# Moving the exponentials and the shares of a tile's expert choice to later rows of the plan

## What is computed

```python
q = (ht @ peer_wq).reshape(T, PEER_HEADS, PEER_DK)            # T = 512, 8 heads
s1, s2 = q[..., :half] . peer_k1, q[..., half:] . peer_k2     # 128 scores each
v1, i1 = lax.top_k(s1, 16);  v2, i2 = lax.top_k(s2, 16)
cand = (v1[..., :, None] + v2[..., None, :]).reshape(T, 8, 256)
sc, pos = lax.top_k(cand, 16)
experts = (e1 * 128 + e2)                                     # e1, e2 from i1, i2 by pos
gates = jax.nn.softmax(sc, axis=-1)
a = jax.nn.gelu(einsum("ckd,cd->ck", peer_u[experts], h)) * gates
out = einsum("ck,ckd->cd", a, peer_v[experts])
```

## Time and profile before

| | us |
|---|---|
| runs before: median of 3 (lowest, highest) | 2980.7 (2978.4, 2987.61) |
| the profiled execution, its own time | 2978.2 |
| its span, first to last instruction | 2976.5 |
| TensorE busy in the span | 2824.8 (95%) |
| VectorE busy | 2235.7 (75%) |
| ScalarE busy | 1481.7 (50%) |
| GpSimd busy | 582.0 (20%) |

### The profile page before, as it was taken

One profiled execution on the slowest core, in us unless ns is written; L12 is line 12 of the kernel. 1 busy time (PEld: TensorE's weight loads), 2 busy tenths in 40 slices (PEclk: granted clock), 3 DMA queues, 4 the chain that ended last, 5 costly groups with the idle time before them and its releaser, 6 DMA issues.

```text
span 2976.5 us, 37320 instructions
## 1 busy us (share of the span) xinstructions
PE 2824.8 (95%) x13639; PEld 2359.7 (79%) x13639; DVE 2235.7 (75%) x3019; ACT 1481.7 (50%) x1990; POOL 582.0 (20%) x460
## 2 busy tenths in 40 slices
PE   5989987999999989999999999899999999999998
PEld 3666756888888857776777789899999998888887
DVE  6465546888888863696964599999777658888886
ACT  3433235888888843544552333555665633333332
POOL 0200111111111100000000000233333324444442
PEclk7999998999999999999999999999999999999999
DMA  7544635999999833232334324688998999999995
GB/s 305 171 160 146 212 137 205 368 372 367 363 360 352 324 140 128 86 114 89 117 106 149 114 86 142 236 293 308 322 319 310 326 337 358 368 364 357 362 371 174
DMA packets 201771, 737.90 MB, mean 248 GB/s; under 512 B 24432, under 2 KB 77808, under 8 KB 145008
## 3 DMA queue, kind: packets, MB, share of 16 engines
q1 hardware_dynamic: 124656, 497.12, 46.3%
q0 software_dynamic: 55056, 170.87, 16.7%
q10 hardware_dynamic: 21872, 67.48, 5.9%
HBM read 666.61 MB, written 93.91 MB: 256 GB/s over the span
## 4 chain that ended last, share of the span: by engine, by line
PE 64%; DVE 13%; issue 4%; ACT 2%; DMA 1%; ACTq 0%; DVEq 0%; SPq 0%; POOLq 0%
PE PS L544 55%; DVE wlo L1891 3%; PE PS L1145 2%; PE PS L1011 1%; PE PS L1023 1%; DVE hf L2700 1%; ACT whi L1221 1%; PE PS L850 1%; DVE oh L2674 1%; DVE hf L2688 1%; ACT HH L1861 1%; DVE cand L2640 1%; DVE cand L2642 1%; PE PS L1002 1%; DVE sS L2727 0%
## 5 line engine op out<-in xcount | busy, mean ns | idle before, releaser
L1891 DVE TENSOR_TENSOR wlo<-raw,whi 128x2048 fp32r<-128x2048 f32 x392 | 894.2, 2289 | 311.9 <-ACT whi L1221 270.9
L1221 ACT ACTIVATE whi<-raw 128x2048 fp32r<-128x2048 f32 x392 | 750.7, 1916 | 371.5 <-PE PS L544 317.3
L544 PE MATMUL PS<-HH,whi 128*128 128x512 f32 (+1 forms) x2056 | 787.8, 383 | 20.1 <-ACT HH L1257 10.1
L544 PE MATMUL PS<-HH,wlo 128*128 128x512 f32 (+1 forms) x2056 | 750.6, 365 | 0.0
L544 PE MATMUL PS<-HL,whi 128*128 128x512 f32 (+1 forms) x2056 | 750.3, 365 | 0.0
L544 PEld LDWEIGHTS PS<-HH,whi 128*128 128x128 f32 x2056 | 390.5, 190 | 78.1 <-issue 20.4
L544 PEld LDWEIGHTS PS<-HL,whi 128*128 128x128 f32 x2056 | 390.6, 190 | 46.6 <-issue 7.7
L544 PEld LDWEIGHTS PS<-HH,wlo 128*128 128x128 f32 x2056 | 389.3, 189 | 43.3
L544 PE MATMUL PS<-whi,HH 128*128 128x512 f32 (+1 forms) x896 | 350.6, 391 | 11.1 <-DVE HL L2730 5.8
L544 PE MATMUL PS<-whi,HL 128*128 128x512 f32 (+1 forms) x896 | 346.8, 387 | 0.0
L544 PE MATMUL PS<-wlo,HH 128*128 128x512 f32 (+1 forms) x896 | 346.8, 387 | 0.0
(11 more groups left out here) (434 smaller groups left out, 3891.9 us busy)
## 6 DMA issues: line engine op xcount, KB each, us to landing
raw<-in_moe_dram SPq DMA_DIRECT2D x192, 1024.0 KB, 7.2
raw<-in_u_units_dram SPq DMA_DIRECT2D x64, 1024.0 KB
raw<-in_v_units_dram SPq DMA_DIRECT2D x64, 1024.0 KB
raw<-in_w_in_dram SPq DMA_DIRECT2D x44, 1024.0 KB
raw<-in_w_ada_dram SPq DMA_DIRECT2D x24, 1024.0 KB, 20.1
acts_dram<-sS ACTq DMA_DIRECT2D x64, 384.0 KB
gates_dram<-XT ACTq DMA_DIRECT2D x24, 1024.0 KB
sS<-acts_dram SPq DMA_DIRECT2D x42, 384.0 KB
```

Of the source, the lines that this page charges most:

```text
L544: ins = t.matmul(dst, a, b, start=(first and n == 0), stop=(last and n == 2))
L1221: a.inc(a.e.activation(m.whi[p % HRING][:, :, :], m.raw[RAW_SLOT[load_of(p)]][:, :, :], ACT.Copy), "hi", p)
L1891: v.inc(v.e.tensor_tensor(m.wlo[h][:, :, :], m.raw[RAW_SLOT[load_of(p)]][:, :, :], m.whi[h][:, :, :].bitcast(F32), ALU.subtract), "lo_v", p)
```

## The change

The share (r = 9) leaves the list of choice steps, which has nine steps for a tile instead of ten. The planner puts the exponential of a tile three rows after its subtraction (`EXP_AFTER`) and its share four rows after it (`SHARE_AFTER`), as entries 3 and 4 of a row. ScalarE does the exponential after the row's gate steps instead of before them; VectorE does the share after the row's gate steps and before its choice steps. The gate steps hang on the row of the share instead of that of the last choice step. The rule that a tile's first step may not stand in the row in which the tile before it was finished is gone.

```diff
--- before.py
+++ after.py
@@ -157,7 +157,8 @@
 
 
 CHOICE_ORDER = (1, 0, 2, 3)
-CHOICE_NS = (1500, 4600, 4600, 2000, 3400, 3400, 3400, 3400, 800, 700)
+CHOICE_NS = (1500, 4600, 4600, 2000, 3400, 3400, 3400, 3400, 800)
+EXP_AFTER, SHARE_AFTER, SHARE_NS = 3, 4, 700
 N_PAIR = 4 * 16 + 12 * 4
 CHOICE_STEPS = len(CHOICE_NS)
 N_GATE = 32 * (NT - TD // 128)
@@ -172,15 +173,16 @@
 
 
 def peer_schedule():
-    up, chosen, a, b, c = [], {}, 0, 0, 0
+    up, chosen, shared, a, b, c = [], {}, {}, 0, 0, 0
     tensor, vector = 0, FOUND_NS
     for n in range(128):
-        row = ([], [], [])
+        row = ([], [], [], [i for i in chosen if n == chosen[i] + EXP_AFTER], [i for i in shared if n == shared[i]])
         tensor += 4200
         vector = max(vector, tensor - 4200) + 1150
-        first = chosen.get(TD // 128, n)
+        vector += SHARE_NS * len(row[4])
+        first = shared.get(TD // 128, n)
         while (b * (LAST_GATE - first) < GATE_STEPS * (n - first) and b < GATE_STEPS and len(row[1]) < 2
-               and (b >= N_GATE or n > chosen.get(TD // 128 + b // 32, n))):
+               and (b >= N_GATE or n > shared.get(TD // 128 + b // 32, n))):
             row[1].append(b)
             b += 1
             tensor += 1100
@@ -192,13 +194,11 @@
             c += 1
         while a < CHOICE_STEPS * NT and vector < tensor + 2000:
             i, r = choice_of(a)
-            if r == 0 and a and n == chosen[choice_of(a - 1)[0]]:
-                break
             row[0].append(a)
             vector += CHOICE_NS[r]
             a += 1
             if r == CHOICE_STEPS - 1:
-                chosen[i] = n
+                chosen[i], shared[i] = n, n + SHARE_AFTER
         up.append(row)
     assert a == CHOICE_STEPS * NT and b == GATE_STEPS
     down = [list(range(c + (256 - c) * min(n, 124) // 124, c + (256 - c) * min(n + 1, 124) // 124))
@@ -1778,12 +1778,10 @@
     a.mark("scored")
 
 
-def act_choice_step(a, m, step):
-    i, r = choice_of(step)
-    if r == 8:
-        a.wait_ge("gsub", i)
-        dst = m.act0[:, :] if i * 128 < TD else m.gt[:, i, :, :].rearrange("p h k -> p (h k)")
-        a.inc(a.e.activation(dst, dst, ACT.Exp), "gexp5", i)
+def act_choice_exp(a, m, i):
+    a.wait_ge("gsub", i)
+    dst = m.act0[:, :] if i * 128 < TD else m.gt[:, i, :, :].rearrange("p h k -> p (h k)")
+    a.inc(a.e.activation(dst, dst, ACT.Exp), "gexp5", i)
 
 
 def act_gate_step(a, m, step):
@@ -1844,10 +1842,10 @@
         u, ci = divmod(n, 2)
         if ci == 0:
             act_high(a, m, FIRST["u_units"] + u + HRING - 1)
-        for step in PEER[n][0]:
-            act_choice_step(a, m, step)
         for step in PEER[n][1]:
             act_gate_step(a, m, step)
+        for i in PEER[n][3]:
+            act_choice_exp(a, m, i)
         for step in PEER[n][2]:
             act_gather_step(a, m, step)
         activation(n)
@@ -2652,13 +2650,18 @@
             v.inc(e.tensor_copy(m.IDX[:, :].rearrange("p (h k) -> p h k", h=8), m.e12[:, :, :]), "index")
         v.inc(e.tensor_tensor(G3, m.sc16[:, :, :], bass.AP(m.sc16, 0, [[128, 128], [16, 8], [0, 16]]),
                               ALU.subtract), "gsub", i)
-    elif r == 9:
-        v.wait_ge("gexp5", i)
-        v.inc(e.tensor_reduce(m.gs[:, :], G3, AX.X, ALU.add), "pick")
-        v.own()
-        v.inc(e.reciprocal(m.gs[:, :], m.gs[:, :]), "pick")
-        v.own()
-        v.inc(e.tensor_tensor(G3, G3, bass.AP(m.some, 16, [[32, 128], [1, 8], [0, 16]]), ALU.mult), "gt", i)
+
+
+def dve_choice_share(v, m, i):
+    e = v.e
+    dst = m.act0[:, :] if i * 128 < TD else m.gt[:, i, :, :].rearrange("p h k -> p (h k)")
+    G3 = dst.rearrange("p (h k) -> p h k", h=8)
+    v.wait_ge("gexp5", i)
+    v.inc(e.tensor_reduce(m.gs[:, :], G3, AX.X, ALU.add), "pick")
+    v.own()
+    v.inc(e.reciprocal(m.gs[:, :], m.gs[:, :]), "pick")
+    v.own()
+    v.inc(e.tensor_tensor(G3, G3, bass.AP(m.some, 16, [[32, 128], [1, 8], [0, 16]]), ALU.mult), "gt", i)
 
 
 def dve_gate_step(v, m, step):
@@ -2709,6 +2712,8 @@
             dve_low(v, m, FIRST["u_units"] + n // 2 + HRING - 1)
         for step in PEER[n][1]:
             dve_gate_step(v, m, step)
+        for i in PEER[n][4]:
+            dve_choice_share(v, m, i)
         for step in PEER[n][0]:
             dve_choice_step(v, m, step)
         for step in PEER[n][2]:
```

## The result

| | before | after |
|---|---|---|
| median of 13 runs each (lowest, highest), us | 2983.2 (2978.37, 2988.09) | 2973.51 (2968.78, 2977.18) |
| the profiled execution, its own time | 2978.2 | 2970.07 |
| its span | 2976.5 | 2968.3 |

The ratio is 0.9966, with a 95% interval of 0.9959 to 0.9973: faster by 10.1 us (8 to 12). Forecast were a gain of 12.3 us and a time of 2968.4. The time was missed by 5.1: the runs before now have a median 2.5 us higher than 2980.7, and the medians differ by 9.7 instead of 12.3.

The account below looks back on a forecast made before the run. TensorE sets the pace, but VectorE, full from row 12 to 57, limits its gain: 4.2 at product 57, plus 8.6, less 0.5, makes 12.3 us off the profiled 2978.2; median expected 2968.4 us, range 2958 to 2980.

Parts of the forecast that it names:

- The waits removed: Choice rows: no exponential waits for VectorE's backlog any more; ScalarE had waited 32.0 us for subtractions, VectorE 5.6 for exponentials.
- VectorE decides, at product 57: Tightest place: TensorE gains only VectorE's advance plus spare, less gate steps, 4.2 us at most of 15.3 us of stops.
- The size of the advance: VectorE by row 57: 3.9 us of waits plus 3.7 of one-hots less 2.5 for gathered rows, 5.1 us ahead.
- the spare: At product 57: room between ScalarE's gate copy and TensorE's last multiply, 1.8 us.
- What comes back as short stops: Products 26 to 57: TensorE waits again for low halves and gate copies, 11.1 us; sign, some 8 to 12 us idle.
- The stop of 6.27 us: After product 58: the stop goes with its lowered clock, 8.6 us gained, 0.5 given back at row 59.
- The moved steps and the table loads: First steps of tiles 0, 2, 3 and exponentials of 2.9 us in busy rows: no term of their own.
- The change of phase: Before the down units: last gate step 5.05 us later leaves the gates' read 8.3 us; slower rival, 2986 us, chance 0.04.
- Full recovery: Rival: TensorE gets back all 23.9 us of stops, 2956.8 us; chance 0.13, nearly full recovery included.
- Most of it eaten: Rival: VectorE's advance is nothing at product 57, the end gains 7.2 us, 2973.5 us; chance 0.20.
- Slower clock in pieces: Rival: many short stops hold the granted clock down, ten slow gate groups cost 11.6 us, 2980 us; chance 0.05.

Follow-up runs that it names:

- experiment 2: The changed kernel with every gather step one row later, first in row 23; median 2968.79 us, ratio 0.9943.
- experiment 3: The changed kernel with the planner's TensorE times set to 4160 and 890 ns, choices ending in rows 12, 22, 43, 65; median 2963.74 us, ratio 0.9931.
- experiment 1: The kernel before with only the gate steps begun four rows later, exponentials and shares left in place; median 2984.66 us, ratio 1.0002.
- experiment 4: The changed kernel with VectorE's product of one-hots and indices left out for tiles 2 and 3, 10 us less work; one run, 2961.52 us.
- experiment 6: The changed kernel with the exponential one row and the share two rows behind the subtraction, instead of three and four; median 2972.12 us, ratio 0.9969.
- experiment 7: The changed kernel with its last gate step in row 121 instead of 119; one run, 2975.56 us.
- experiment 8: The changed kernel with both TensorE's planner times at 4160 and 890 ns and every gather step one row later; median 2962.49 us, ratio 0.9944.
- experiment 5: The kernel before with VectorE's product of one-hots and indices left out for tiles 2 and 3, 10 us less work; one run, 2972.69 us.

## Why the prediction was right, step by step

The gains at the start of a product against the same product before, both from the start of product 0, in us. Up to row 119 a part of it is only that after has fewer gate steps behind it, 0.89 us each; the fourth column takes it off; the last two are as measured.

| product | after | gate steps behind | after, net | one row later (2) | other times (3) |
|---|---|---|---|---|---|
| 28 | 9.6 | 4 | 6.1 | 16.1 | 13.2 |
| 57 | 5.20 | 3 | 2.5 | 12.3 | 14.4 |
| 60 | 12.45 | 3 | 9.8 | 19.6 | 22.95 |
| 127 | 9.75 | 0 | 9.8 | 16.9 | 20.3 |

**The waits removed.** Right. In after ScalarE has no wait for a subtraction, VectorE none for an exponential, and the granted clock between 2060 and 2100 is 1.00, where it was 0.82 between 2081 and 2100 in the earlier trace rows. The later gate steps by themselves change the time by nothing (experiment 1): they put VectorE ahead, but TensorE can't use it behind the old exponentials.

**VectorE decides, at product 57.** Right in place and kind. Net of the gate steps, TensorE gained 6.1 us by product 28, had 2.5 of them left at 57, and won 7.3 more by product 60. Experiments 2 and 4 show the cause from both sides: VectorE 7.2 us further ahead gave 7.2 of gain, and less work on VectorE took away every stop behind product 28. And what TensorE has gained at the start of product 58 follows VectorE's advance at the low half of row 57, whatever stops and lowered clock lie before it: 4.4 us with an advance of 3.0 in after, 11.6 with 10.1 in experiment 2, 4.0 with 2.6 in experiment 6, 1.4 to 1.5 more each time.

**The size of the advance.** This is the mis-sized term: 5.1 us predicted. The low half of row 57 begins at 2081.71 us before and at 2080.36 after, so with the 1.62 us between the starts of product 0 VectorE was 3.0 ahead. The two lines, before and then after:

```profile
2081.71 2.28 DVE L1891 TENSOR_TENSOR wlo<-raw,whi 128x2048 fp32r<-128x2048 f32 x1
```

```profile
2080.36 2.29 DVE L1889 TENSOR_TENSOR wlo<-raw,whi 128x2048 fp32r<-128x2048 f32 x1
```

Of the missing 2.1, 1.5 are the gather's. I had VectorE idle for 3.8 us, with 7.8 from the index to the landing of the second block as before. It was 5.3, with 9.3. From after, the index and the two dots on VectorE, and the two fetches on GpSimd:

```profile
1888.81 0.23 DVE L2650 CAST IDX<-e 128x128 uint32<-128x128 f32 x1
...
1895.35 1.23 DVE L2691 CUSTOM_DVE_ANT_0 hf<-sq,hN 128x1024 f32<-128x1024 f32 x1 [3.51 <-DMA sq<-in_peer_u_dram,IDX]
...
1898.37 1.22 DVE L2691 CUSTOM_DVE_ANT_0 hf<-ht,hN 128x1024 f32<-128x1024 f32 x1 [1.79 <-DMA ht<-in_peer_u_dram,IDX]
```

```profile
1889.89 1.30 POOL L3028 DMA_INDIRECT sq<-in_peer_u_dram,IDX  x1 [85.07 <-DVE i16f L2621]
1891.50 1.23 POOL L3028 DMA_INDIRECT ht<-in_peer_u_dram,IDX  x1 [0.30 <-issue]
```

The rest, about 0.6 us, I can't name; experiment 1, which moves only the one-hots, has VectorE 2.9 ahead in place of the 3.7 that I gave them, so it may lie there. With 3.0 in place of 5.1 the prediction's own sum, 1.8 + 3.0 - 2.7 + 8.6 - 0.5, is 10.2 us; 9.8 were measured. Of the 0.4, 0.3 is the spare: 1.4 to 1.5 by the three runs above, where the prediction had 1.8.

**What comes back as short stops.** Right: 8.6 us of them, where 8 to 12 were forecast, at gate copies and low halves, almost all between products 26 and 57. Behind the stop of 2.77 us the clock fell, which the last section prices at 1.6 us. That needs no term in the sum: it lies before product 57, where TensorE stands at VectorE in any case. In experiment 6 the stop in row 27 was 4.46 us, with the clock at 0.50 in the 4 us behind it, and TensorE had gained 7.3 us at product 28 instead of 9.6; at product 58 it was 4.0 instead of 4.4, as much less as VectorE's advance.

**The stop of 6.27 us.** Right: 8.6 - 0.5 = 8.1 predicted. The net gain rises by 7.3 from product 57 to 60, or by 8.0 from its low point at product 58.

**The moved steps and the table loads.** Right, but for half a microsecond. TensorE has no stop before product 26, though (0,0) and (0,1) put the low half of row 13 back by 5.2 us. The exponential of tile 0 in row 24 stands between its two loads without a gap, by the timeline of ScalarE. The prediction counted none of its 2.9 us; the gate copy behind the second load ends at 1908.23 us, and TensorE's stop of 0.47 at 1908.37 waits for it. It lies before product 57, so the sum doesn't change.

```profile
1903.04 1.28 ACT L1817 ACTIVATE oh<-oh,eT 128x128 f32<-128x128 f32 x4 [6.59 <-DVE oh L2677]
1904.34 1.28 ACT L1784 ACT_TABLE_LOAD   x1
1905.63 0.31 ACT L1784 ACTIVATE act<-act 128x128 f32<-128x128 f32 x1
1905.96 1.28 ACT L1835 ACT_TABLE_LOAD   x1
```

The load begins 0.02 us after the scalings end, and the exponential 0.01 us after the load. The Trainium skill (ScalarE: Activation LUTs, What ACT_TABLE_LOAD costs) adds a drain of about 1.38 us to each load: these rows show none.

**The change of phase.** Right: the stop of TensorE remained 2.92 us, and experiment 7, with 7.1 us less from the gates' read to the first down multiply, left it at that too.

**The rivals.** Full recovery (23.9 us) is out for this kernel, but experiment 3 gets 20.3 of it with one other plan: the limit is where the plan puts VectorE's work. "Most of it eaten" had the advance at nothing: it was 3.0. "Slower clock in pieces" is out: 1.6 us of it in after, and none that reaches the end.

## What to carry to other kernels

When a wait is taken out between two engines that are both nearly full, the stops behind it come back as far as the other engine doesn't get ahead: here 23.9 us of stops gave 9.8. Work that out at the tightest later row, and don't add up the stops. Then look for idle time on the engine that decides: here one line took away 5.3 us of VectorE's idle before two dots and put one dot later, and was worth 7.2 us. And put measured times into a planner before its order is tuned by hand: two constants (1100 to 890, 4200 to 4160 ns) gave 10 us more, as much as the change itself, though in part the same 10 as that one line.

## What the runs showed of the hardware

**A stop of 2 to 3 us costs clock in some executions and none in others.** Behind the 2.77-us stop of after, multiplies of 128x384 took 0.53 us instead of 0.34, up to 1905.9; of such lines as

```profile
1902.70 0.53 PE L544 MATMUL PS<-HL,whi 128*128 128x384 f32 x1
...
1905.59 0.53 PE L544 MATMUL PS<-HL,whi 128*128 128x384 f32 x1
...
1906.32 0.34 PE L544 MATMUL PS<-HL,whi 128*128 128x384 f32 x1
```

there are ten, 3.2 us, at the level of 1.2 GHz. Half of that time, 1.6 us, is lost; the window above has 0.58 for 4 us, which makes 1.7. The same came behind shorter stops: 2.60 us in experiment 4 (clock 0.65 in the 4 us from its end) and, in experiment 7, 2.09 (0.69; ten such multiplies again):

```profile
1904.16 0.44 PE L544 MATMUL PS<-HH,whi 128*128 128x384 f32 x1 [2.09 <-DVE wlo L1889]
```

The stop of 3.08 us in experiment 3 is followed by none; its clock is 1.00 from 1900 to 1940. And the same stop of 2.92 or 2.93 us at the change of phase is followed by 1.00 in seven of the ten traces, after among them, and by 0.93 in experiment 1, 0.85 in experiment 7 and 0.91 in experiment 8, in the 20 us behind it. Windows of after and of experiment 8:

```profile
2423.18:2443.18 20.00, 20.00 (x88) 16.56 (x89) 14.16 (x15) 6.25 (x5) 4.46 (x4) 1.00 0.92 315
```

```profile
2413.18:2433.18 20.00, 20.00 (x81) 16.40 (x82) 12.99 (x14) 5.99 (x5) 3.16 (x3) 0.91 0.93 319
```

By the share of the 20 us that is missing, experiments 7 and 8 lose 3.0 and 1.8 us there. The prediction said that behind short stops no fall shows. In these traces that held for every stop of up to 1.8 us; of those of 2.09 to 3.19 us some are followed by a fall and some not, and every one of 4.46 us or more is.

**The first fetch by index.** GpSimd's first two took 1.30 and 1.23 us to issue in after and in experiments 2, 4, 6 and 7, 1.08 and 1.01 in before and in experiments 1 and 5, and 1.23 and 1.02 in experiments 3 and 8, the same to 0.01 us within each family. In before VectorE was waiting for the exponential beside the first of them, in after it was at work. Whether that slows GpSimd no run here tells. It isn't what made the rows land late in after, for in experiment 6, with the same 1.30 and 1.23, the second block was used 7.8 us behind the index, as in before:

```profile
1898.74 1.23 DVE L2691 CUSTOM_DVE_ANT_0 hf<-ht,hN 128x1024 f32<-128x1024 f32 x1 [1.02 <-DMA ht<-in_peer_u_dram,IDX]
```

VectorE's idle before the first two dots was 3.8 us there, what the prediction had. It was 4.6 in experiment 7 and 5.2 in experiment 4, whose plans are that of after up to these dots, with 8.7 and 9.2 us from the index, and 5.3 with 9.3 in after. So the landing of the same two fetches varies by over half a microsecond between executions; what it depends on stays open.
